# A one-core transformer pair on Trainium2: the loading order and the tiling of the opening stage

## The reference

```python
mod_l = (jax.nn.silu(c) @ w_mod[l] + b_mod[l])[:, None, :]
mod_c = (jax.nn.silu(c_ctx) @ w_mod[l] + b_mod[l])[None, None, :]
sh1, sc1, g1, sh2, sc2, g2 = jnp.split(mod_l, N_MOD, axis=-1)
sh1c, sc1c, g1c, sh2c, sc2c, g2c = jnp.split(mod_c, N_MOD, axis=-1)
pl = _modulate(_rmsnorm(xl, norm1_w[l]), sh1, sc1) @ w_in[l]
pc = _modulate(_rmsnorm(xc, norm1_w[l]), sh1c, sc1c) @ w_in[l]
```

## Time and profile before

| what | value |
|---|---|
| median of 3 runs | 3248.41 us |
| the runs | 3248.42, 3248.41, 3242.74 us |
| profiled execution, device time | 3245.03 us |
| its span in the trace | 3243.2 us |
| PE busy / DVE / ACT / POOL | 97% / 42% / 18% / 64% |

### The profile page before, as it was taken

The page is one execution under the profiler, slowest core; times in us unless marked ns, Lnnn a source line. Parts: engine busy times, 40 slices in busy tenths (PEclk is TensorE's granted clock), DMA queues, the critical chain, the costliest instruction groups (busy, mean ns, idle before and its releaser), DMA issues.

```text
span 3243.2 us, 39373 instructions
## 1 busy us (share of the span) xinstructions
PE 3141.9 (97%) x14911; PEld 2562.9 (79%) x14911; DVE 1361.8 (42%) x1615; ACT 587.6 (18%) x966; POOL 2061.1 (64%) x1475
## 2 busy tenths in 40 slices
PE   4999988999999999999999999999999999999998
PEld 3867967788888888876888888888888768888887
DVE  4944256688544331333335332333322343343321
ACT  3154264212111100112102110111001120011100
POOL 2442466588877776633667776777776336777774
PEclk7989998999999999999999999999999999999999
DMA  6120244223233223321233332323233212233322
GB/s 201 46 65 27 66 125 128 91 91 103 81 102 101 93 83 97 128 78 52 78 99 96 100 94 85 109 91 102 84 90 125 76 53 91 91 96 98 99 81 80
DMA packets 350001, 298.21 MB, mean 92 GB/s; under 512 B 6596, under 2 KB 347588, under 8 KB 349640
## 3 DMA queue, kind: packets, MB, share of 16 engines
q1 hardware_dynamic: 346616, 290.49, 28.7%
q10 hardware_dynamic: 3280, 6.26, 0.6%
HBM read 292.53 MB, written 2.10 MB: 91 GB/s over the span
## 4 chain that ended last, share of the span: by engine, by line
PE 91%; DVE 5%; POOL 1%; issue 1%; ACT 1%; DMA 1%; DVEq 0%; SPq 0%; POOLq 0%; ACTq 0%
PE pm L1999 24%; PE pm L2000 24%; PE pm L2001 24%; PE pa L1999 2%; PE pa L2001 2%; PE pa L2000 2%; DVE cacc L1350 2%; PE pa L2488 1%; PE pa L2501 1%; PE pm L2045 1%; PE pm L2266 1%; PE pm L2047 1%; PE pm L2046 1%; POOL wlo L590 1%; PE pa L2226 1%
## 5 line engine op out<-in xcount | busy, mean ns | idle before, releaser
L590 POOL TENSOR_TENSOR wlo<-raw,whi 128x512 fp32r<-128x512 f32 (+1 forms) x1096 | 1441.6, 1347 | 22.8
L586 POOL TENSOR_SCALAR whi<-raw 128x2048 fp32r<-128x2048 f32 (+1 forms) x274 | 482.3, 1760 | 1097.3 <-PE pm L2001 642.5
L1999 PE MATMUL pm<-hh,whi 128*128 128x512 f32 x2408 | 945.9, 393 | 18.8 <-DVE hl L1306 15.7
L2000 PE MATMUL pm<-hl,whi 128*128 128x512 f32 x2408 | 938.5, 390 | 0.0
L2001 PE MATMUL pm<-hh,wlo 128*128 128x512 f32 x2408 | 938.3, 390 | 0.0
L1999 PEld LDWEIGHTS pm<-hh,whi 128*128 128x128 f32 x2408 | 452.9, 188 | 122.9 <-issue 19.5
L2000 PEld LDWEIGHTS pm<-hl,whi 128*128 128x128 f32 x2408 | 453.0, 188 | 95.4 <-issue 2.4
L2001 PEld LDWEIGHTS pm<-hh,wlo 128*128 128x128 f32 x2408 | 452.9, 188 | 94.8
L1999 PE MATMUL pm<-uh,whi 128*128 128x512 f32 x880 | 343.0, 390 | 0.7 <-POOL wlo L590 0.7
L2001 PE MATMUL pm<-uh,wlo 128*128 128x512 f32 x880 | 342.4, 389 | 0.0
L2000 PE MATMUL pm<-ul,whi 128*128 128x512 f32 x880 | 342.3, 389 | 0.0
(11 more groups left out here) (428 smaller groups left out, 3887.1 us busy)
## 6 DMA issues: line engine op xcount, KB each, us to landing
raw<-in_w_ffn SPq DMA_DIRECT2D x88, 1024.0 KB, 5.3
raw<-in_w_in SPq DMA_DIRECT2D x62, 1024.0 KB, 5.2
raw<-in_w_ffn SPq DMA_DIRECT2D x64, 704.0 KB, 4.6
raw<-in_w_up SPq DMA_DIRECT2D x22, 1024.0 KB, 5.1
raw<-in_w_mod SPq DMA_DIRECT2D x20, 1024.0 KB, 7.3
raw<-in_w_out SPq DMA_DIRECT2D x12, 1024.0 KB, 5.4
raw<-in_w_down SPq DMA_DIRECT2D x16, 704.0 KB, 4.6
modraw<-in_w_mod SPq DMA_DIRECT2D x4, 1024.0 KB, 12.1
```

The costliest lines, as they stand in the source:

```text
L586: nc.gpsimd.tensor_scalar(h, r, 1.0, 1.0, ALU.mult, ALU.mult).then_inc(hi_done, 1)
L590: last = nc.gpsimd.tensor_tensor(o[:, c], r[:, c], h[:, c].bitcast(F32), ALU.subtract)
L1999: nc.tensor.matmul(out, wh, ah, start=start, stop=False)
L2000: nc.tensor.matmul(out, wh, al, start=False, stop=False)
```

## The change

1. **Loads.** SP loads x before the context, then the first slab of `w_in` into `raw[0]`, then the first 2048 columns of `w_mod` as eight k tiles of 128 x 2048 (8 KB in a row) into eight buffers of their own (`modraw`, over the arena of later tiles and the head of `hl`); nothing of it waits. The second `w_in` slab follows without a wait.
2. **Modulation on PE.** A k tile is four matmuls of 512 columns, one for each of the four groups of 32 array columns, all into bank `pm[1][:, 0]`, summed over k in PSUM. Group g then holds columns 512g to 512g + 511, and nothing is left to add. PE waits for the k tiles in pairs. ACT copies 512 columns instead of 2048, `mod_turn` is 4 matmuls with 8 columns instead of 16 with 2, with columns of `ident` in place of `modsel`; DVE adds the bias in one instruction instead of two.
3. **Root mean square.** PE adds the eight squares itself (eight matmuls against `ones` that accumulate in `pa[n]`), and DVE has no part in it. x comes first. 1/rms and the scaled tile (once `hn`) lie in PSUM: `pa[n]` and `pa[2 + k % 2]`.
4. **Normalisation.** The eight k tiles of x come first, those of the context after them. The four ones columns of `mv` are set later on POOL, since `modraw` lies there first.
5. **HGRN stage.** The other 4096 columns of `w_mod` come as 16 k tiles of 2048 columns through `raw[0]` and `raw[1]`. PE does one k tile on each of the levels 0 to 7 and 11 to 18 (`MOD_AT`), and turns 16 tiles on levels 9 and 20. Rows and biases are made twice instead of eight times.

```diff
-MOD_GAP = 3
+MOD_AT = (0, 11)
...
-            sp.dma_start(cx[:], io["ctxT"].rearrange("(k p) t -> p k t", p=P)).then_inc(ctx_loaded, 16)
             sp.dma_start(x[:], io["xT"].rearrange("(k p) t -> p k t", p=P)).then_inc(x_loaded, 16)
-            for i in range(MOD_FIRST):
-                b = i % len(modraw)
-                if i >= len(modraw):
-                    sp.wait_ge(mod_used, i - len(modraw) + 1)
-                sp.dma_start(modraw[b][:], wm[:, :, SLAB * i:SLAB * i + SLAB]).then_inc(mod_loaded[b], 16)
+            sp.dma_start(cx[:], io["ctxT"].rearrange("(k p) t -> p k t", p=P)).then_inc(ctx_loaded, 16)
+            sp.dma_start(raw[0][:], slab_view(io["w_in"], 0, IN1[0][1])).then_inc(raw_loaded[0], 16)
+            for k in range(KD):
+                sp.dma_start(modraw[k][:], wm[k][:, 0:MOD_W]).then_inc(mod_loaded[k // 2], 16)
...
+            for i in range(KD, MOD_LOADS):
+                if i < KD + 2:
+                    sp.wait_ge(split_done, OUT1_AT + i - KD - 1)
+                else:
+                    sp.wait_ge(mod_used, i - 1)
+                sp.dma_start(raw[i % 2][:].rearrange("p k n -> p (k n)"), wm[i % KD][:, MOD_W * (i // KD):MOD_W * (i // KD) + MOD_W]).then_inc(mod_loaded[i % 2], 16)
...
-            pool.wait_ge(mod_used, MOD_FIRST)
             for i, (name, _) in enumerate(IN1):
+                if i == 1:
+                    pool.wait_ge(mod_used, KD)
+                    nc.gpsimd.memset(mv[:, :, :, HEAD_DIM:], 1.0).then_inc(mv_ones, 1)
                 split(2 + i, i % 2, i // 2 + 1, KD // 2 * P if name == "gate" else 8 * SLAB)
...
+                for n, (src, loaded, w) in enumerate(((x, x_loaded, T), (cx, ctx_loaded, CT))):
+                    act.wait_ge(loaded, 16)
+                    act_squares(act, n, src, w)
+                    act.wait_ge(sq_added, 8 * n + KD)
+                    nc.scalar.activation(std[:, 0:w], pa[n][:, 0:w], ACT.Ln, bias=eps[:], scale=1.0 / D).then_inc(std_done, 1)
+                    act.wait_ge(std_done, n + 1)
+                    nc.scalar.activation(pa[n][:, 0:w], std[:, 0:w], ACT.Exp, scale=-0.5).then_inc(rstd_done, 1)
...
+                act.wait_ge(mod_used, KD)
+                nc.scalar.activation(modrow[0][:], pm[1][:, 0, :], ACT.Copy).then_inc(mod_row, 1)
...
+                for n, (src, hi, lo, w) in enumerate(((x, hh, hl, T), (cx, ch, cl, CT))):
...
+                        nc.vector.scalar_tensor_tensor(pa[2 + k % 2][:, 0:w], src[:, k, :], wsc[:, n, k:k + 1], pa[n][:, 0:w], ALU.mult, ALU.mult).then_inc(hn_done, 1)
...
+                    for g in range(4):
+                        last = nc.tensor.matmul(out[32 * g:32 * g + 32, :], silc[:, k, :], src[:, T * g:T * g + T], start=k == 0, stop=k == KD - 1)
+                    last.then_inc(mod_used, 1)
+                    yield
...
+                    for r, at in enumerate(MOD_AT):
+                        if at <= n < at + KD:
+                            next(rest)
+                        if n == at + KD + 1:
+                            pe.wait_ge(mod_row, r + 2)
+                            mod_turn(modrow[1], pm[0][:, 1, :])
...
+                for n, w in enumerate((T, CT)):
+                    for k in range(KD):
+                        pe.wait_ge(sq_done, 8 * n + k + 1)
+                        nc.tensor.matmul(pa[n][:, 0:w], ones[:], sq[k % 2][:, 0:w], start=k == 0, stop=k == KD - 1).then_inc(sq_added, 1)
```

More of the change, by code:

```diff
@@ L146, in build @@
         rstd = place("rstd", [P, T], F32, scratch + 3 * TILE)
-        hn = [place(f"hn{b}", [P, T], F32, scratch + (4 + b) * TILE) for b in range(2)]
         ident = place("ident", [P, P], F32)
@@ L301, in build @@
         mod_loaded, mod_used, mod_in, mod_done, lb_step, lb_exp = (
-            [sem(f"mod_loaded{b}") for b in range(6)], sem("mod_used"), sem("mod_in"), sem("mod_done"), sem("lb_step"), sem("lb_exp"))
+            [sem(f"mod_loaded{k}") for k in range(KD // 2)], sem("mod_used"), sem("mod_in"), sem("mod_done"), sem("lb_step"), sem("lb_exp"))
         ctx_free = [sem("ctx_free0"), sem("ctx_free1")]
@@ L1249, in dve_square @@
                 nc.vector.tensor_tensor(acc, acc, sq[i][:, 0:W], ALU.add).then_inc(sq_added, 1)
-        def dve_squares(v, n, W=T):
-            for k in range(KD):
-                dve_square(v, n, k % 2, 8 * n + k + 1, k == 0, W)
         def dve_low(v, n, k, gain):
@@ new lines, in first, with scaled, low @@
+                for n, (src, hi, lo, w) in enumerate(((x, hh, hl, T), (cx, ch, cl, CT))):
+                    nc.vector.scalar_tensor_tensor(wsc[:, n, :], modc[:, KD:2 * KD, n], 1.0, cols("norm1", 0, KD), ALU.add, ALU.mult).then_inc(mod_done, 1)
+                    v.wait_ge(mod_done, n + 2)
+                    v.wait_ge(rstd_done, n + 1)
+                    def scaled(k):
+                        if 8 * n + k >= 2:
+                            v.wait_ge(hl_done, 8 * n + k - 1)
+                        nc.vector.scalar_tensor_tensor(pa[2 + k % 2][:, 0:w], src[:, k, :], wsc[:, n, k:k + 1], pa[n][:, 0:w], ALU.mult, ALU.mult).then_inc(hn_done, 1)
+                    def low(k):
+                        v.wait_ge(hh_done, 8 * n + k + 1)
+                        nc.vector.scalar_tensor_tensor(lo[:, k, :], pa[2 + k % 2][:, 0:w], mod_col(0, k, n), hi[:, k, :].bitcast(F32),
+                                                       ALU.add, ALU.subtract).then_inc(hl_done, 1)
+                    for k in range(KD):
+                        scaled(k)
+                        if k:
+                            low(k - 1)
+                    low(KD - 1)
@@ L2012, in norm @@
                 pe.wait_ge(sq_added, 8 * n + KD)
-                nc.tensor.matmul(pa[0][:, 0:W], ones[:], (std if n else cstd)[:, 0:W], start=True, stop=True).then_inc(sq_summed, 1)
+                nc.tensor.matmul(pa[0][:, 0:W], ones[:], std[:, 0:W], start=True, stop=True).then_inc(sq_summed, 1)
             def two_norms():
@@ L2153, in in1 @@
                 else:
-                    last = slab_first(b, p, 1) if i == 0 else slab_t(b, hh, hl, p, KD)
+                    last = slab_first(b, p, 0) if i == 0 else slab_t(b, hh, hl, p, KD)
                     if name in ("mk", "zf", "zb"):
+                        pe.wait_ge(hl_done, 2 * KD)
                         last = context_t(b, p)
@@ L2187, in mlstm @@
             def mlstm():
+                pe.wait_ge(mv_ones, 1)
                 pe.wait_ge(pm_free[0], IN1_USE[6] + 1)
```

202 lines of the change are left out of this document (63 added, 139 removed).

## The result

The changed kernel takes 3226.11 us (median of 4 runs, 3225.26 to 3227.05), the kernel before 3246.44 (median of 4, the three runs of the table above and one more, 3242.74 to 3248.42). The ratio is 0.9939, 95% interval 0.9922 to 0.9956: 0.6% less time, 20.3 us where 17.0 were forecast. The profiled execution took 3225.26 us with a span of 3223.5; before, 3245.03 and 3243.2.

What follows compares the result with a forecast made beforehand. PE is 91% busy, so time is won where it waits, runs at low clock or drops work. Opening 15.7 - 4.9 + 3.2 = 14.0 plus HGRN 3.0 gives 17.0 off 3248.4: 3231.4 us, range 3224 to 3243 (8 in 10).

Steps and rivals of the forecast that it cites:

- The sum: Whole kernel: opening 14.0 us won plus HGRN stage 3.0 makes 17.0, median 3231.4; chance 0.62.
- Landing of the last k tile: Opening loads: x and context, `w_in` slab, k tiles at 395 GB/s and a tail land at 40.7, between 39.7 and 43.6.
- From landing to x: Opening: last two tiles 3.9 us, row copy 0.6, turn 1.75, bias and `wsc` 1.2; x starts at 48.2, 15.7 earlier.
- Root mean square hidden, PSUM operands free: Opening: PE's ones matmuls end near 28, before the fifth tile lands; PSUM operands on DVE cost nothing.
- From x to the first tap: Opening: context tiles now behind x add 7.5 us, pad fills and copy 1.3; 20.8 for 15.9, 4.9 given back.
- POOL beside the taps: Convolution start: POOL's slab 2 split falls 70 per cent on the context, sparing 3.5 of five slow taps, 3.2 us won.
- HGRN stage: Fewer turns win 2.4 us, smaller blocks and fewer waits 1.5, loads lose 1; 3 won, between 7 won and 4 lost.
- half of these will be: nothing: HGRN stage: modulation tiles, 0.97 us on each of 16 levels, half on the chain as before, so no net change.
- Rival 1: Opening gives half: PE's low clock, or k tiles at 348 GB/s and slower x; 14.0 shrinks to 4 to 9; chance 0.15.
- rival 2: More than the sum: k tiles above 395 GB/s, HGRN blocks vanish in PE's idle time; 3 + 4 more, 3224; chance 0.12.
- rival 3: HGRN levels wait for loads, PE in order behind them: 39 us lost against 14 won, 3273; chance 0.05.
- rival 4: Nothing carries over: a later stage tied to something that does not move loses the gain, 3247; chance 0.06.

Runs made afterwards that it cites:

- levels: Changed kernel with the 16 k tiles of the HGRN stage at spaced levels, one level free after two tiles: 3220.19 us, ratio to before 0.9922.
- second_late: Changed kernel with the first eight HGRN tiles still on levels 0 to 7 and the second eight packed on levels 16 to 23: 3223.11 us.

## Why the prediction was nearly right

The sum stood at 17.0 us, 20.3 were measured. Its own range, 3227 to 3236 against a median of 3248.4, is 12 to 21 us won, and holds that. The opening won more than forecast, by steps that were mis-sized, and the HGRN stage won nothing where 3 us were forecast. By its steps:

- **Landing of the last k tile.** 40.7 forecast, 38.67 measured: 2.0 us of the missing gain. Two terms failed. The rate, 395 GB/s from the row with 2 KB, pointed the right way and stopped at the last row that there was; tiles with 8 KB ran at 420 to 423, 1.4 us less. And the tail of 1.3 us did not come back. It was read from the kernel before, where PE took the last three slabs from 33.23, 36.24 and 40.63, so the last one came 4.4 us after the one ahead, against 3.0; hardly anything moved from 38 to 40 us (stretch of the kernel before, columns as in the earlier trace rows), though that load had been issued at 28.52. Now the last tile comes at the pace of the others, with more loads issued behind it. Why the queue paused before is open. Against these, the `w_in` slab was in at 18.7, 0.5 later than the 18.2 of the sum.

```profile
38.00:40.00 2.00, 0.18 (x4) 0.00 (x0) 0.00 (x0) 0.00 (x0) 0.00 (x0) 0.50 0.29 45
```

 By the rule of the Trainium skill that was weighed ("DMA: Bandwidth & Descriptors", section "Where 436 GB/s comes from") the rate would have been 358. The 420 measured speaks against using that rule for one core by itself; the table in the section "Bandwidth" of the same page of the Trainium skill, 425 GB/s for 16 MB with the neighbouring core idle, is the part of it with which this trace agrees.
- **From landing to x.** 7.5 forecast, 6.0 measured: 1.5 more. The last pair took 3.60 at the low clock (3.9). The turn was put at a quarter of 7.00, 1.75; it took 1.06, in a stretch with the clock back at 0.97, where the 7.00 had been at 0.50. Bias and `wsc` took 0.54 for 1.2. Two of these are luck: the other eleven kernels with this pair ran it in 1.92, and in nine of them `wsc` alone took 1.0 to 1.1, for 0.17 here.
- **Root mean square hidden, PSUM operands free.** Both held: the matmuls against `ones` were over at 29.8 (near 28 forecast), and the context's instructions took 0.49 beside POOL. The kernels that take these steps back found nothing in the opening for the first and 7 to 9 us for the second.
- **From x to the first tap.** 20.8 forecast, 20.7 measured, against 15.9 before.
- **POOL beside the taps.** 3.2 us forecast; first tap to fourth images took 63.0 for 66.5, 3.5 won. The slow taps went from five to two: the first took 0.50 for 1.72 and two more 0.76 for 1.68, 3.1 us. That the order matters by this and not by the 11.3 us of the context is what the kernel with the context first measured (4 to 6 us).
- **HGRN stage.** 3 us won were forecast, 0.3 lost, and this is the step whose account failed. Spaced tiles have the stage 5.6 us shorter than before, so there was more to win than the 2.4 and 1.5 of the sum; what failed is the term set against it, 1 us for loads. The packed placing costs some 6 us against the spaced one. PE waited for loads 7 times for just under 1 us, since two levels take at least 6.1 us (the prediction had 6.2 to 7.6); the 2.8 us of the first group cost nothing up to the twelfth level, and 1.9 us are in the second. The larger part was no term at all: two groups on eight levels in a row leave levels bare behind each, where PE waits for DVE and goes on at a lower clock. By PE's busy time that is some 4 us. The prediction's "half of these will be: nothing" took tiles as a cost only; by these profiles they are also what keeps PE's clock up where they stand.
- **Not in the sum.** From the last head's product to the end the changed kernel takes 1.3 us less, 2697.6 for 2698.9. The code there is the same, and the other twelve kernels take 2697.4 to 2700.3, so this is scatter.

The opening gave 4.0 us more than forecast up to the fourth images (18.0 for 14.0) and 0.8 behind them, the HGRN stage 3.4 less, and 1.3 came at the end by chance: the misses partly cancelled, and that the total is so near is in part luck. Rival 1 fell with the landing and the ones matmuls; rival 2 was right about the rate of the k tiles and wrong about the HGRN stage; rival 3's wait was there, 4.7 us in all for 39; rival 4 is excluded by the table.

## What to carry to other kernels

Optional work that is spread over a stage should be spread over all of it: packed tight it meets its own loads, and behind it the engine idles and loses its clock. When instructions of DVE are put beside POOL's, look where their tensor inputs lie: one in PSUM kept them at 0.75 us where two in SBUF took 1.7. And a load that goes ahead of the one that the chain waits for delays it by its full length, 3.2 us here, of which some 2 reached the end because nothing waited for what it started early. Last, one profile of each kernel is not enough for effects of 2 us: the same code took 98.0 to 102.3 us in the same stage.

## What the runs showed of the hardware

- **Row length sets the rate of a load, above 395 GB/s too.** On one queue of one core: 347 to 350 GB/s with rows of 1 KB, 395 with 2 KB, 420 over 20 us with 8 KB.
- **DVE beside POOL.** The slow-down follows the operands: 1.64 to 1.85 us for 0.75 with two inputs in SBUF, none with one in PSUM. Two inputs are not needed for it: the first tap, one tensor input and its output in SBUF, takes 0.48 by itself and took 1.70 beside POOL before, 1.45 in "levels" and 1.52 in "second_late". It looks like a wait and not like half speed. In "levels" the tap runs from 64.18 to 65.63, and the instruction of POOL beside it ends at 65.35; in the changed kernel that instruction ends 0.1 us after the tap's start, and the tap takes 0.48. The eight-column product `wsc` shows the same: it took 1.0 to 1.1 us in nine of the kernels, each time ending within 0.03 us of the end of POOL's first instruction of a split (43.47 and 43.46 in "levels"), and 0.17 in the changed one, where it began only as that instruction ended.
- **The clock of the last pair is not fixed by the code in front of it.** The changed kernel's pair was run at 1.2 GHz, that of "second_late", with the same instructions ahead and the same gap, at 2.4 GHz (PE's timeline of the one, then of the other). The 1.7 us between them scatter from profile to profile. The pair took 1.92 to 1.93 us in all eleven other kernels that have it, idle matmuls or not, so what idle matmuls do for it is not shown.

```profile
38.67 3.60 PE L2134 MATMUL pm<-modraw,silc 128*32 128x512 f32 x16 [3.06 <-DMA modraw<-in_w_mod]
```

```profile
37.89 1.92 PE L2135 MATMUL pm<-modraw,silc 128*32 128x512 f32 x16 [3.08 <-DMA modraw<-in_w_mod]
```
